# Gates, key-value block and MLA output in another order, and a network's first tanh ahead of its fourth unit's rounding

## The reference

```python
x = first_block(x, ...)                       # retention, block attention, network 0
for i in range(2):
    if i == 1:                                # from the stream as layer 0 leaves it
        h = x @ kv_w_down                     # 256 latent columns and 64 rope columns
        c_kv = rms_norm(h[..., :256], kv_norm)
        k_rope = rope(h[..., 256:], cos, sin)
        kv = einsum('bsc,chd->bshd', c_kv, kv_w_up)       # keys and values of 16 heads
    x = post_norm(x, 0.5 * swiglu(x, ffn1_w_in[i], ffn1_w_out[i]), ...)
    mix = fox_mixer(x, ...) if i == 0 else mla_mixer(x, ...)
    x = post_norm(x, mix, ...)
    x = post_norm(x, 0.5 * swiglu(x, ffn2_w_in[i], ffn2_w_out[i]), ...)
    gate = sigmoid(x @ ple_w_gate[i] + ple_b_gate[i])
    x = post_norm(x, gate * (p[i] @ ple_w_proj[i]), ...)
```

## Time and profile before

| | us |
|---|---|
| three runs | 1565.73, 1565.86, 1567.34 |
| their median | 1565.86 |
| the profiled execution | 1565.49 |
| its span, first to last instruction | 1563.5 |
| TensorE busy in it | 1517.2 |
| VectorE, ScalarE, POOL busy | 933.9, 783.6, 182.8 |

### The profile page before, as it was taken

How to read it: one execution, slowest core, us unless ns; L and a number is a source line. 1 busy time by engine, 2 the same in 40 slices (tenths; PEclk the granted TensorE clock), 3 DMA queues, 4 the chain that set the end, 5 groups by cost and what they waited for, 6 DMA issues and landing times.

```text
span 1563.5 us, 22063 instructions
## 1 busy us (share of the span) xinstructions
PE 1517.2 (97%) x8444; PEld 1315.5 (84%) x8444; DVE 933.9 (60%) x1214; ACT 783.6 (50%) x935; POOL 182.8 (12%) x54
## 2 busy tenths in 40 slices
PE   8999999999999999899999999899999999999997
PEld 6888888888888888798888888788888887888885
DVE  7475465666656667214666667766666355666667
ACT  5436444444444444655454446554446554544455
POOL 0014211000010001350100002100005441100001
PEclk9999999999999999999999999999999999999999
DMA  8444345655565554532555555565554334555552
GB/s 311 168 141 170 140 162 187 216 192 188 183 193 189 189 190 159 163 134 86 175 199 188 190 193 197 171 202 190 191 192 161 103 112 164 172 199 188 188 201 81
DMA packets 186861, 274.35 MB, mean 175 GB/s; under 512 B 9953, under 2 KB 137057, under 8 KB 186722
## 3 DMA queue, kind: packets, MB, share of 16 engines
q1 hardware_dynamic: 182848, 261.72, 50.2%
q10 hardware_dynamic: 3954, 11.80, 2.3%
HBM read 272.44 MB, written 1.05 MB: 175 GB/s over the span
## 4 chain that ended last, share of the span: by engine, by line
PE 83%; DVE 9%; ACT 4%; issue 1%; DMA 1%; POOL 0%; ACTq 0%; SPq 0%; DVEq 0%
PE bank L652 22%; PE bank L654 12%; PE bank L525 6%; PE bank L527 6%; PE bank L526 6%; PE acc L525 6%; PE acc L526 6%; PE acc L527 6%; DVE w_lo L1561 3%; PE acc L787 2%; ACT w_hi L1132 2%; PE acc L521 2%; PE bank L576 1%; PE bank L570 1%; PE bank L583 1%
## 5 line engine op out<-in xcount | busy, mean ns | idle before, releaser
L1561 DVE TENSOR_TENSOR w_lo<-w_raw,w_hi 128x2048 fp32r<-128x2048 f32 (+2 forms) x210 | 477.1, 2276 | 181.6 <-ACT w_hi L1210 121.6
L652 PE MATMUL bank<-xT,w_hi 128*128 128x512 f32 x1520 | 380.2, 392 | 2.0 <-DVE hid L1705 1.2
L480 POOL TENSOR_TENSOR w_lo<-w_raw,w_hi 128x2048 fp32r<-128x2048 f32 (+2 forms) x42 | 176.7, 4211 | 1345.6 <-ACT w_hi L1132 1345.6
L652 PEld LDWEIGHTS bank<-xT,w_hi 128*128 128x128 f32 x1520 | 276.1, 189 | 53.9 <-DVE hid L1705 1.6
L1210 ACT ACTIVATE w_hi<-w_raw 128x2048 fp32r<-128x2048 f32 x145 | 276.5, 1907 | 0.0
L654 PEld LDWEIGHTS bank<-xT,w_lo 128*128 128x128 f32 x1520 | 207.4, 190 | 14.8
L654 PE MATMUL bank<-xT,w_lo 128*128 128x256 f32 x1520 | 211.9, 282 | 0.0
L1132 ACT ACTIVATE w_hi<-w_raw 128x2048 fp32r<-128x2048 f32 (+4 forms) x107 | 191.8, 1817 | 27.9 <-DMA w_raw<-in_w_in 7.8
L525 PE MATMUL acc<-w_hi,hTh 128*128 128x512 f32 x400 | 156.2, 391 | 0.0
L526 PE MATMUL acc<-w_lo,hTh 128*128 128x512 f32 x400 | 156.2, 391 | 0.0
L527 PE MATMUL acc<-w_hi,hTl 128*128 128x512 f32 x400 | 155.6, 389 | 0.0
(11 more groups left out here) (221 smaller groups left out, 2145.9 us busy)
## 6 DMA issues: line engine op xcount, KB each, us to landing
w_raw<-in_ffn_w_in SPq DMA_DIRECT2D x176, 512.0 KB, 4.4
w_raw<-in_ffn_w_out SPq DMA_DIRECT2D x88, 512.0 KB, 4.2
w_raw<-in_w_in SPq DMA_DIRECT2D x52, 512.0 KB, 4.8
w_raw<-in_fox_w_in SPq DMA_DIRECT2D x24, 512.0 KB, 4.5
w_raw<-in_w_ffn_gate SPq DMA_DIRECT2D x22, 512.0 KB, 4.7
w_raw<-in_w_ffn_up SPq DMA_DIRECT2D x22, 512.0 KB, 4.5
w_raw<-in_w_ffn_down SPq DMA_DIRECT2D x22, 512.0 KB, 3.9
w_raw<-in_ple_w_gate SPq DMA_DIRECT2D x16, 512.0 KB, 4.1
```

The costliest lines, as they stand in the source:

```text
L480: pool.tensor_tensor(w_lo[s][:, 0:cols], w_raw[u % RING][:, 0:cols], w_hi[s][:, 0:cols].bitcast(F32), ALU.subtract).then_inc(w_lo_done[u % ...
L652: pe.matmul(out, wh[:, k, m], both, start=k == 0, stop=False)
L1561: nc.vector.tensor_tensor(w_lo[s][:, 0:cols], w_raw[u % RING][:, 0:cols], w_hi[s][:, 0:cols].bitcast(F32), ALU.subtract).then_inc(w_lo_don ...
```

## The change

Four edits of order; no instruction's size changes.

1. In all networks ScalarE splits unit u0+2, takes the first tanh, and then splits u0+3; VectorE runs what is due in the middle (`mid`, the latent's rest) after that split. At the end of networks 2 and 4 one more unit is split before the last hidden tile is rounded and a second ahead of the root table, in network 1 two ahead of the root table.
2. In both layers the gates run tile by tile: the projections take banks 0 to 3, the transposes banks 4 to 7, and tile 0 has both column halves done before the last half of tile 1. ScalarE and VectorE follow. `kv_down` runs tile 0 ahead of network 3 and tile 1 inside its first product; `turn_ckv` stands behind the first `wide`. POOL no longer splits `kv_down`'s two units and network 3's second, and of the gate's first two units it takes the first instead of the second.
3. `kv_up(3)` stands ahead of the first query unit; `kv(3)`'s keys are multiplied before the latent's transposes and its values behind them.
4. `turn_o(7)` is first, then the first unit of both halves of the MLA output for both tiles, `turn_p(1)`, and then the second units tile by tile, each tile's columns complete together.

```diff
-POOL_STAGES = ("ga1", "gb0", "gb1", "kv_down0", "kv_up", "fox_q1", "fox_k1", "fox_q2", "fox_k2", "fox_v5", "fox_q3", "fox_k3", "uq",
+POOL_STAGES = ("ga1", "gb0", "gb1", "kv_up", "fox_q1", "fox_k1", "fox_q2", "fox_k2", "fox_v5", "fox_q3", "fox_k3", "uq",
...
     kv_up(2)
-    uq(0)
     kv_up(3)
-    for g in range(1, 8):
+    for g in range(8):
         uq(g)
...
-    for c in range(2):
-        for k0 in (8, 12):
+    for k0 in (8, 12):
+        for c in range(2):
             dense(f"mla_ob{c}", w["mla_w_o"], k0, 4, c * CH, CH)
...
-    pool_units |= {unit_at[f"ffn{f}"][0] + 1 for f in range(5)}
+    pool_units |= {unit_at[f"ffn{f}"][0] + 1 for f in (0, 1, 2, 4)}
...
-                                                      ("ple_g00", 1), ("ple_g10", 1))}
+                                                      ("ple_g00", 0), ("ple_g10", 0))}
...
-                if src is None:
-                    start()
+                if kv_down:
+                    to_xT(site, x, tiles=(1,))
+                    for b in (0, 2):
+                        take(b, ("ffn_out", f, 0))
+                    first(0, 0, parts=0)
+                    kv_down.run(0, 1, tiles=(1,))
+                    first(0, 0, parts=1)
+                    first(0, 1)
+                    first(1, 0)
+                    first(1, 1)
...
                     kv(2)
+                    kv(3, values=False)
                     for t in range(T):
                         need("pe", "cqn", t)
...
+                    kv(3, keys=False)
...
                     uq(0)
-                    kv(3)
                     uq(1)
...
+                    turn_o(7)
                     need("pe", "oT", 4)
                     need("pe", "oT", 5)
-                    ob[0]()
-                    turn_o(7)
+                    ob0.run(0)
+                    ob1.run(0)
+                    turn_p(1)
                     need("pe", "oT", 6)
                     need("pe", "oT", 7)
-                    ob[1]()
-                    ob[2]()
-                    chunk("mla_ob1", (2, 3), slot0=8)
-                if l:
-                    turn_p(1)
+                    for t in range(T):
+                        ob0.run(1, tiles=(t,))
+                        ob1.run(1, tiles=(t,))
...
                 ple_p(0)
-                to_xT(4 + 4 * l, x, between=between)
-                ple_g[1]()
-                ple_g[2]()
-                chunk(f"ple_g{l}1", (2, 3))
+                to_xT(4 + 4 * l, x, tiles=(0,))
+                ple_p(1)
+                g0.run(0, tiles=(0,))
+                to_xT(4 + 4 * l, x, tiles=(1,))
+                g0.run(1, tiles=(0,), part=0)
+                g0.run(0, tiles=(1,))
+                g0.run(1, tiles=(0,), part=1)
+                g1.run(0, 1, tiles=(0,))
+                g0.run(1, tiles=(1,))
+                g1.run(0, 1, tiles=(1,))
                 if l == 0:
-                    kv_down = tile_steps("kv_down0", (4, 5), ready=5)
-                    to_xT(5, x, between=kv_down[0])
-                    kv_down[1]()
-                    kv_down[2]()
+                    kv_down = Chunk("kv_down0", (4, 5), ready=5)
+                    to_xT(5, x, tiles=(0,))
+                    kv_down.run(0, 1, tiles=(0,))
...
                     if last:
+                        split[0] = u0 + 3 * FI
+                        if f in (2, 4):
+                            split_to(u0 + 3 * FI + 1)
                         hT_round(i, None, hLh)
                         return
...
+                split_to(u0 + 3)
+                first_tanh(u0 + 1)
                 split_to(u0 + 4)
-                first_tanh(u0 + 1)
...
+                if f in (1, 2, 4):
+                    split_to(u0 + 3 * FI + 2)
                 if f:
                     root_table()
-                split[0] = u0 + 3 * FI
-                split_to(u0 + 3 * FI + (2 if f == 1 else 1))
+                split_to(u0 + 3 * FI + 1)
...
+                def finish_ple(t):
+                    if t:
+                        ple_gate(1, 1)
+                        split_to(u0 + 7)
+                    ple_add(1, t)
+
+                ple_gate(0, 0)
+                split_to(u0 + 6)
+                ple_add(0, 0)
                 ple_gate(1, 0)
-                norm_and_turn(5 + 4 * l, lambda t: ple_add(1, t), middle=lambda: ple_gate(1, 1))
+                norm_and_turn(site + 1, finish_ple, centred=lambda: ple_gate(0, 1), scaled=lambda: ple_add(0, 1),
+                              late=lambda: split_to(u0 + 8))
```

More of the change, by code:

```diff
@@ L622, in unit_steps, with to_xT @@
                 return [(lambda w=w: c.run(w)) for w in range(len(c.us))]
-            def to_xT(site, src, qs_=(0, 1), b0=0, between=None):
-                for t in range(T):
+            def to_xT(site, src, qs_=(0, 1), b0=0, between=None, tiles=range(T)):
+                for t in tiles:
                     if t and between:
@@ L665, in last_up, with first @@
                     mm.then_inc(w_used, 1)
-                def first(b, t, ks=range(KD)):
+                def first(b, t, ks=range(KD), parts=None):
                     u = u0 + b
@@ L913, in turn_ckv, with kv @@
                         mm.then_inc(pe_done, mark("pe_done", "ckvTf", t))
[L915 to L917 removed]
+                if l == 0:
+                    ffn(1, "raw", x)
+                else:
+                    ffn(3, 5, mid=turn_ckv, kv_down=kv_down)
+                def kv(c, keys=True, values=True):
                     u = unit_at["kv_up"][c]
@@ L924, in kv @@
                         need("pe", "ckvT", t)
-                    for i in range(2):
+                    for i in range(2 if keys else 0):
                         take(i, ("kT", c, i))
@@ L931, in kv @@
                         mm.then_inc(pe_done, mark("pe_done", "kTf", c, i))
+                    if not values:
+                        return
                     for t in range(T):
@@ L1403, in _, with keep_kv @@
                 ffn(1 + 2 * l, keep_ckv if l else None)
-                def keep_kv(c):
+                def keep_kv(c, keys=True, values=True):
                     ahead("kv_up", c)
-                    for i in range(2):
+                    for i in range(2 if keys else 0):
                         need("act", "kTf", c, i)
@@ L1410, in keep_kv @@
                            bank[i].rearrange("p (h n) -> p h n", h=2))
-                    for t in range(T):
+                    for t in range(T if values else 0):
                         need("act", "vf", c, t)
@@ L1633, in mean @@
                         "mean", site, t)
+                    if t == 0 and centred is not None:
+                        centred()
                     settle()
@@ L1636, in mean @@
                         dve.wait_ge(gb_loaded, gb_count(site))
-                    else:
+                    elif site not in (4, 8):
                         rest(0, 0)
@@ L1674, in norm_and_turn @@
                 mean(0)
-                if middle is not None:
-                    middle()
+                if scaled is not None:
+                    scaled()
                 inverse(0)
@@ L1978, in _ @@
                 if l == 1:
-                    ahead("kv_down0")
+                    split_to(unit_at["ffn3"][0] + 2)
                     for t in range(T):
```

138 lines of the change are left out of this document (79 added, 59 removed).

## The result

The changed kernel takes 1551.87 us (median of 4 runs, 1550.2 to 1552.92) where the kernel before, in runs beside it, takes 1565.80: a ratio of 0.9912 with a 95% interval of 0.9900 to 0.9923. Run again later beside three experiments it took 1549.88 against 1565.83, a ratio of 0.9896 (0.9881 to 0.9911). It is 14 to 16 us faster; 1554.0 was forecast, with a range from 1547.5 to 1560.

A forecast was written before the change was run, and what follows sets the result against it. TensorE, busy 97% of the span, was taken as the bound, with 46 us of waits to gain. Terms 2.75 + 7.1 − 2.8 + 2.6 + 1.95 = 11.6 off 1565.49 gave 1554.0 us; range 1547.5 to 1560.

The forecast's parts named there:

- part 2: Layer 0's gates, kv_down and network 3's start: tile-by-tile order cuts TensorE's waits; 7.1 us gained, between 5 and 8.5.
- part 5: Layer 1's last gates and tail: waits of 1.4 and the first tile's apply go; 1.95 us gained, 1.3 to 2.3.
- part 1: Networks' starts: first tanh ahead of the fourth unit's rounding removes three waits, 2.75 us; networks' ends nothing, ±0.4 each.
- 8.4, less 0.57 and 0.6: Network 3's first wide: 8.4 us early, less 0.57 for the latent's turn and 0.6 for possible clock falls.
- Part 3: MLA front: POOL's roundings in a row hold VectorE's root steps, TensorE waits 4.0; −2.8 us, between +2.2 and −5.
- Rival B: MLA front: small root steps slip between POOL's roundings, +2.2 in place of −2.8; 1549.0 us, chance 0.2.
- Rival D: Networks' starts: the rounding moved behind the tanh is read too late, +2.75 becomes −13.5; 1570.1 us, chance 0.04.
- the cover of 3 us: Networks' starts: the fourth unit's rounding, about 2.5 us later, still precedes its reading by the up half's wide product.
- Part 4: MLA output and next site: waits of 1.41 and 0.88 covered, 0.75 left; 2.6 us gained, 1.8 to 3.2.
- Rival C: Layer 0's gates and MLA front: clock falls after waits lose 2.5 and 2 us more; 1558.5 us, chance 0.18.
- Rival E: Gates: VectorE, with 7.5 us more, becomes late behind each root, and the front costs 5; 1562.8 us, chance 0.03.

The follow-up runs named there:

- run 5: Kernel before with only the networks' first tanh moved ahead of the rounding of u0+3: 1561.71 us, ratio 0.9976.
- run 3: Changed kernel with ScalarE's order at the networks' start put back, both units rounded ahead of the first tanh: 1553.34 us, ratio 0.9929.
- runs 4, 6: In the order named: changed kernel with only network 1's end put back, 1551.99 us; kernel before with only that end changed, 1563.22 us.
- run 11: Kernel before with only the ends of networks 1, 2 and 4 as in the changed kernel: 1561.69 us, ratio 0.9973.
- run 10: Kernel before with the gates tile by tile and the new ends of networks 1, 2 and 4: 1553.72 us, ratio 0.9921.
- run 9: Changed kernel with tanh order, network ends, MLA front and MLA output put back, leaving the gates alone: 1561.84 us, ratio 0.9978.
- run 1: Changed kernel with the MLA front put back, first query unit ahead of kv_up(3): 1548.56 us, ratio 0.9898.
- 8 against 12: Changed kernel with the MLA output's order put back, 1552.96 us, against the changed kernel run again in the same rounds, 1549.88 us.
- run 12: Changed kernel again, unedited, beside three other experiments: 1549.88 us, ratio 0.9896.
- run 2: Changed kernel with only the residual of kv_up(3) moved from POOL to VectorE: 1544.79 us, ratio 0.9876.
- run 7: Changed kernel with kv_down's two units and network 3's second unit rounded by POOL again: 1551.02 us, ratio 0.9909.

## Why the prediction was right, and where it was not

The sum was 11.6; measured are 13.9 and, in the second comparison, 15.9.

| part | forecast | by traces | by runs that isolate it |
|---|---|---|---|
| 1, first tanh | 2.75 | 2.7 (run 5), 2.6 (run 3) | 3.8 (run 5, a fall of the clock included) |
| 1, ends of networks | 0, ±0.4 each | network 1: 1.5 (runs 4, 6, 11); layer 0's gates 1.4 and last gates 1.3 without part 2 (11), 3.6 and 1.85 with it (10 against 9) | 4.1 (11), 8.4 (10 against 9, the clock at 625 included) |
| 2, gates, kv_down, ffn3 | 7.1 | 7.2; 3.5 without the ends | 3.7 with part 5, without the ends (run 9) |
| 3, MLA front | −2.8 | −3.0 | −3.3 by the trace of run 1 |
| 4, MLA output | 2.6 | 3.2 | 3.1 (8 against 12) |
| 5, last gates and tail | 1.95 | 1.95, of which 1.3 come with the ends alone; 0.2 without the ends | in run 9 |

**The step that failed** is the sentence of part 1 on the ends of the networks: "the load of these units or the chain of the norm ends last there, and I take nothing, ±0.4 a network". The chain of the norm does end last, and that is why they pay: VectorE's queue holds the residual of the very unit that ScalarE rounds late, in front of the norm's adding. What it cost stood in the kernel before's list of waits:

```profile
PE acc L525 <- DVE x L1611: 2.0, 2, 1.0
```

These are a wait of 1.01 at 952.38 and one of 1.04 at 1527.70, each in front of a product of the projection of p, until VectorE has done the adding of the norm's second tile. Run 11, which has the new ends alone, has neither. In the kernel before the ends were worth 1.5 us at network 1, 1.4 at network 2 and 1.3 at network 4 (run 11); with the gates tile by tile the last two were worth 3.6 and 1.85 (run 10 against 9).

The forecast of part 2 was near in size (first product to first wide: 53.3 forecast, 53.8 measured, and 52.75 in run 12 without a fall of the clock) only because I counted TensorE's queue from its start with no waits up to the gates, and so took the ends' work for granted without costing it. Run 9 shows the gain that the gates have without it: 3.5 there and 0.2 in the tail. Inside the sum two errors also met: I took 4.3 of waits where 2.4 stand (1.47, 0.78 and 0.18), and the work between them, with its restarts, takes some 1.3 more than by my prices. (From 8.4, less 0.57 and 0.6, the sum of part 2 would be 7.2 and not 7.1.)

**Part 5** hit 1.95 by luck. I put it down to the gates' order. But from the last wide product to TensorE's end it takes 48.35 before, 48.88 with the gates alone (run 9), 47.03 with the ends alone (run 11) and 47.03 with both (run 10). So 1.3 of it is the ends' work, and the gates' order brings only the 0.65 behind TensorE's last product (6.45 for 7.08).

**Network 1's end** brings 1.5, for which the sum had nothing. The other 1.6 of what the two traces differ by there are the clock's windows at 0.73 and 0.93, which the kernel before had in the one trace from which I read. I had such a fall in view at 980 to 990 and not here. The two together are most of what the forecast is short of.

**Part 3** went as written: the root step held to the end of the second residual (3.26), the small steps caught twice, a wait of 3.2 for the 4.0 forecast (the steps were held once between 1197.37 and 1199.95 and once more from 1200.80, with four short ones in between), and a window at 0.66 behind. That the total fits, −3.0 for −2.8, is in part luck: the wait was taken 0.8 too long, and the clock, taken at 0.8, cost some 1.6 (eight 512-column products stand 0.42 apart there instead of 0.23). Rival B is out. The Trainium skill (SBUF — State Buffer, section "SBUF: two separate sides") speaks of an exclusive lock for a whole instruction; the rows above agree, the 128x2 operations too, and in both directions. In run 2 VectorE's residual of 2.27, begun within one of POOL's, took 5.02; in run 7 POOL's of 4.6, begun 1.0 before the end of one of VectorE's, took 5.58. What could not be read from the rule is that a gap of 0.04 us between two of VectorE's operations is enough for POOL to come in.

**Part 1's tanh:** sum right, distribution a little off: 0.5 instead of 1.0 in network 4, and 0.6 in network 3, where "none" was written: the wait was hidden there by the lateness that part 2 took away. Rival D, the fourth unit read late, didn't show in any trace; the cover of 3 us held.

**Part 4** was 0.5 too low: no wait stands in front of the second tile's transposes where I took 0.75. **Rival C**, the clock, was right as a mechanism and small in size: falls to 0.78 and 0.88 behind the gates in one trace of the changed kernel and none in the other, and one window of about 0.7 behind the front in both. **Rival E** took VectorE as the bound with four roundings more: run 7 gave three of them back to POOL and was not faster.

What stays open is when the clock falls. Up to TensorE's last product, windows below 0.95 stand at 625, 630, 980 and 985 before, at 175, 975, 980 and 1205 in the changed kernel's first trace, at 1205 alone in its second. A fall is worth 1 to 2 us and none of the runs separates it from the order of the work. The 14 to 16 us contain such falls on either side, so the parts of the sum aren't known to better than that.

## What to carry to other kernels

When a stage is reordered so that its chain is read sooner, cost again what stands in front of the chain's first step on each engine, even where it cost nothing before: here the roundings at the ends of networks 2 and 4 were worth 2.7 us in the old order of the gates and 5.4 in the new one. Look in the list of waits first, even for short ones: the two of 1.0 us stood there. And be wary of two long GpSimd operations in a row where VectorE has a chain of short ones on SBUF: here moving one residual of 4.6 us to VectorE shortened that stretch by 5.2 us, where the reordering with both on GpSimd had made it 3.0 longer.

## What the runs showed of the hardware

- A VectorE operation of 0.16 us on 128x2 elements took 2.58 to 3.26 us where a POOL operation was under way or came in, and ended with it; POOL got in between two of VectorE's that stand 0.04 us apart.
- Such a meeting cost only on the path: with three residuals back on POOL next to the gates (run 7) two of VectorE's operations were held by 0.8 and 1.0 us, and only the second moved TensorE, by 0.8.
- Up to TensorE's last product the granted clock lay below 0.95 in none to four windows of 5 us in each of the 14 traces (lowest 0.50), always in the same few places (twice 175, else 625 to 635, 975 to 990 and 1200 to 1215), but not in all traces at each, with the same order of work: a difference of 1 to 2 us between two single traces can be this and nothing else. The two traces of the changed kernel differ by it at 175 and at 975 to 985. In all 14 the clock is also low (0.50 to 0.59 in at least one window) once TensorE has finished, where it costs nothing.
